# GpSimd adds the squares of four norms, and behind three norms TensorE takes two units together, chunk by chunk

## What is computed

```python
def rms_norm(x, g):
    xf = x.astype(jnp.float32)
    y = xf * lax.rsqrt(jnp.mean(xf * xf, axis=-1, keepdims=True) + EPS)
    return (y * g.astype(jnp.float32)).astype(x.dtype)

def modulate(x, g, shift, scale):
    return rms_norm(x, g) * (1 + scale) + shift
```

## Time and profile before

| What | Value |
|---|---|
| Runs | 2468.7 us median of 3 (2468.6 to 2469.37) |
| The profiled execution's own time | 2463.28 us |
| Its span, first to last instruction | 2461.5 us |
| Mean granted TensorE clock | 0.919 |
| TensorE busy with products | 2011.6 us (82%), 16358 instructions |
| VectorE, ScalarE, GpSimd busy | 909.3, 659.1 and 58.4 us |
| Products of line 524 (sums of squares), all norms | 88 instructions |

### The profile page before, as it was taken

One profiled execution on the slowest core, in us unless ns is written; L12 is line 12 of the kernel. 1 busy time (PEld: TensorE's weight loads), 2 busy tenths in 40 slices (PEclk: granted clock), 3 DMA queues, 4 the chain that ended last, 5 costly groups with the idle time before them and its releaser, 6 DMA issues.

```text
span 2461.5 us, 37332 instructions
## 1 busy us (share of the span) xinstructions
PE 2011.6 (82%) x16358; PEld 1478.3 (60%) x16358; DVE 909.3 (37%) x1620; ACT 659.1 (27%) x1143; POOL 58.4 (2%) x83
## 2 busy tenths in 40 slices
PE   6998898999998998999999997766656666666665
PEld 3896555888776885899898454443333333333332
DVE  2345623434523328466475453322211111111112
ACT  4233414323413326454444301111111111111111
POOL 0010100000000001000010000000000000000000
PEclk8998999999999999999999998888888888888888
DMA  8106841222223231343540153999999999999996
GB/s 330 69 35 249 367 172 69 103 103 82 71 92 125 103 117 47 137 174 140 192 174 9 42 221 137 428 426 427 427 427 427 426 427 427 427 428 426 427 428 292
DMA packets 44544, 592.60 MB, mean 241 GB/s; under 512 B 5549, under 2 KB 5737, under 8 KB 8288
## 3 DMA queue, kind: packets, MB, share of 16 engines
q1 hardware_dynamic: 40608, 579.36, 57.5%
q0 software_dynamic: 2992, 8.96, 1.1%
q10 hardware_dynamic: 784, 1.91, 0.2%
HBM read 589.16 MB, written 1.05 MB: 240 GB/s over the span
## 4 chain that ended last, share of the span: by engine, by line
PE 52%; DMA 28%; DVE 6%; ACT 3%; issue 2%; SPq 0%; DVEq 0%; ACTq 0%
DMA s_ring<-in_w_up 12%; PE bank L539 10%; PE bank L541 10%; PE bank L540 10%; DMA s_arena<-in_w_up 8%; PE bank L1152 5%; DMA s_xT<-in_w_up 4%; DMA s_hT<-in_w_up 3%; PE bank L1166 2%; PE bank L593 1%; PE bank L777 1%; PE bank L582 1%; PE bank L1139 1%; DMA s_ring<-in_slabs 1%; PE bank L765 1%
## 5 line engine op out<-in xcount | busy, mean ns | idle before, releaser
L539 PE MATMUL bank<-s_arena_r 128*128 128x256 f32 (+2 forms) x1656 | 549.6, 332 | 39.3 <-DVE s_hT_r L1842 33.5
L1273 ACT ACTIVATE s_arena<-bank 32x256 f32<-32x256 f32 (+7 forms) x439 | 174.0, 409 | 1079.5 <-PE bank L1152 572.1
L541 PE MATMUL bank<-s_arena_r,s_ring_r 128*128 128x512 f32 (+2 forms) x1312 | 443.9, 338 | 0.0
L1152 PE MATMUL bank<-s_ring,s_arena 128*32 128x256 f32 x2048 | 297.6, 507 | 144.4 <-DMA s_xT<-in_w_up 47.4
L540 PE MATMUL bank<-s_hT_r,s_arena_r 128*128 128x512 f32 (+2 forms) x1096 | 369.8, 337 | 0.0
L539 PEld LDWEIGHTS bank<-s_arena_r 128*128 128x128 f32 x1656 | 315.3, 190 | 79.6 <-issue 37.9
L1837 DVE TENSOR_TENSOR s_ring_r<-s_ring,s_arena_r 128x2048 fp32r<-128x2048 f32 (+1 forms) x96 | 232.4, 2425 | 289.6 <-ACT s_arena_r L1273 289.5
L1152 PEld LDWEIGHTS bank<-s_ring,s_arena 128*32 128x32 f32 x2048 | 145.1, 144 | 220.9 <-issue 207.5
L541 PEld LDWEIGHTS bank<-s_arena_r,s_ring_r 128*128 128x128 f32 x1312 | 252.2, 192 | 27.2
L1273 ACT ACTIVATE s_arena_r<-s_ring 128x2048 fp32r<-128x2048 f32 (+1 forms) x96 | 193.2, 2016 | 138.1 <-PE bank L541 137.3
L2420 DVE TENSOR_TENSOR s_arena<-s_arena,bank 64x256 f32<-64x256 f32 x64 | 27.1, 423 | 543.9 <-ACT s_arena L1273 543.9
(11 more groups left out here) (332 smaller groups left out, 2621.9 us busy)
## 6 DMA issues: line engine op xcount, KB each, us to landing
s_ring<-in_slabs SPq DMA_DIRECT2D x72, 2048.0 KB, 8.2
s_ring<-in_w_down SPq DMA_DIRECT2D x32, 2048.0 KB, 28.9
s_ring<-in_w_up SPq DMA_DIRECT2D x32, 2048.0 KB, 32.9
s_ring<-in_w_gate SPq DMA_DIRECT2D x32, 2048.0 KB, 33.4
s_arena<-in_w_gate SPq DMA_DIRECT2D x16, 2048.0 KB, 33.5
s_arena<-in_w_up SPq DMA_DIRECT2D x16, 2048.0 KB, 34.0
s_arena<-in_w_down SPq DMA_DIRECT2D x16, 2048.0 KB, 28.9
s_ring<-in_slabs SPq DMA_DIRECT2D x16, 1408.0 KB, 6.4
```

The costliest lines, as they stand in the source:

```text
L539: mm(out, w_hi_, x_hi_, start=start, stop=False)
L541: return mm(out, w_lo_, x_hi_, start=False, stop=stop)
L1152: last = mm(pb[b][32 * q:32 * q + 32, 0:256], x[:, c, :], w[q // 2][:, c, 256 * (q % 2):256 * (q % 2) + 256], start=c == 0, stop=c == DC - ...
L1273: return act.activation(out, in_, func, **kw)
```

## The change

GpSimd gets `add_squares`: it adds the squares of chunks 0 to 6 in place of the six products, into memory that is free at that time. `residual_norm` then has two products, one of the total and one of chunk 7, both behind the last unit. ScalarE rounds chunk 0 directly behind its modulation and the others as before. `norm_split` interleaves VectorE's factors and splits, two factors ahead, for n2_0 and n2_1. In `ffn` and `in2` TensorE makes the first two units together: three products for each of them whenever a chunk has come.

```diff
+        def sq_sum(name):
+
+            o = AW - W_HALF if name in ("n2_0", "n2_1") else AW - W_OUT - TT
+            return arena[:, o:o + TT]
...
+            def add_squares(name, T):
+
+                q0, _ = norms[name]
+                total = sq_sum(name)[:, 0:T]
+                for c in range(1, DC - 1):
+                    pool.wait_ge(S["sq_ready"], q0 + c + 1)
+                    if c == 1:
+                        pool.tensor_tensor(total, sq[:, q0 % 2, 0:T], sq[:, (q0 + 1) % 2, 0:T], ALU.add).then_inc(S["sq_used"], 2)
+                    else:
+                        pool.wait_ge(S["sq_used"], q0 + c)
+                        pool.tensor_tensor(total, total, sq[:, (q0 + c) % 2, 0:T], ALU.add).then_inc(S["sq_used"], 1)
+            add_squares("n2_0", TT)
+            add_squares("n1_1", TT)
             pool.wait_ge(S["ffn_out_mm"], DC)
             pool.dma_start(meta, d["metaT"].rearrange("(c p) t -> p c t", p=P)).then_inc(S["meta_in"], 16)
...
+            add_squares("n2_1", NT)
+            add_squares("fin", TT)
             pool.wait_ge(S["ffn_out_mm"], 2 * DC)
...
             def residual_norm(name, m, T):
 
-                if m >= 1:
-                    norm_chunk(name, m - 1, DC, 7, T, 1024)
                 if m == DC - 1:
+                    T = TT if name == "fin" else T
+                    pe.wait_ge(S["sq_used"], norms[name][0] + DC - 1)
+                    mm(pb[7][:, 0:T], ON[1024], sq_sum(name)[:, 0:T], start=True, stop=False)
                     norm_chunk(name, m, DC, 7, T, 1024)
...
+                    if i == 0:
+                        for c in range(DC):
+                            pe.wait_ge(S["h_lo"], DC * (2 * l + 1) + c + 1)
+                            for a in range(2):
+                                last = split_mm(pb[a][:, 0:T], w_hi[0][:, c, a, :], wl[:, c, a, :], h_hi[:, c, 0:T], hT_r[:, c, 0:T],
+                                                c == 0, c == DC - 1)
+                                if c == DC - 1:
+                                    last.then_inc(S["ffn_in_mm"], 1)
+                        continue
...
             def in2(slab, units, name, ev, prev, ahead=0):
-                for u in range(units):
+                first = 0
+                if slab == 0:
+                    first = 2
+                    pe.wait_ge(S["w_lo"], W_IN2 + 1)
+                    wh, wl = w_half[0], half(place_r[FIRST["in2"]], 0)
+                    for c in range(DC):
+                        pe.wait_ge(S["h_lo"], 4 * DC + c + 1)
+                        for u in range(2):
+                            last = split_mm(pb[u][:, 0:T2], wh[:, c, 128 * u:128 * u + 128], wl[:, c, 128 * u:128 * u + 128], h2_hi[:, c, :], h2_lo[:, c, :],
+                                            c == 0, c == DC - 1)
+                            if c == DC - 1:
+                                last.then_inc(S[name], 1)
+                for u in range(first, units):
...
                     last.then_inc(S["mod_h"], 1)
-                    if c >= 1:
+                    if c == 0:
+                        h_rounded(2 * l + which, 0, T)
+                    if c >= 2:
                         h_rounded(2 * l + which, c - 1, T)
                 h_rounded(2 * l + which, DC - 1, T)
...
+            def norm_split(name, k, T):
+
+                rsq(name, T)
+
+                def factor(c):
+                    TTn(hT[:, c, 0:T], xT[:, c, 0:T], rstd[:, 0:T], ALU.mult).then_inc(S["mod_xr"], 1)
+                for c in range(2):
+                    factor(c)
+                for c in range(DC):
+                    if c + 2 < DC:
+                        factor(c + 2)
+                    h_rest(k, c, hT[:, c, 0:T], hT_r[:, c, 0:T], h_hi[:, c, 0:T])
+                dve.sem_inc(S["norm_done"], 1)
...
             def ffn(l, T):
-                for c in range(DC):
-                    h_rest(2 * l + 1, c, hT[:, c, 0:T], hT_r[:, c, 0:T], h_hi[:, c, 0:T])
...
-            norm_mod("n2_0", 1, TT)
+            norm_split("n2_0", 1, TT)
...
-            norm_mod("n2_1", 3, NT)
+            norm_split("n2_1", 3, NT)
```

More of the change, by code:

```diff
@@ L551, in ffn @@
                         for c in range(DC):
-                            if i + a == 0:
-                                pe.wait_ge(S["h_lo"], DC * (2 * l + 1) + c + 1)
                             last = split_mm(pb[b][:, 0:T], w_hi[i % 3][:, c, a, :], wl[:, c, a, :], h_hi[:, c, 0:T], hT_r[:, c, 0:T],
@@ L872, in in2 @@
                     for c in range(DC):
-                        if slab + u == 0:
-                            pe.wait_ge(S["h_lo"], 4 * DC + c + 1)
                         last = split_mm(pb[u % 4][:, 0:T2], wh[:, c, o:o + 128], wl[:, c, o:o + 128], h2_hi[:, c, :], h2_lo[:, c, :],
```

## The result

The changed kernel took **2440.2 us** (median of 4 runs, 2436.5 to 2443.6), the kernel before beside it 2468.8: a ratio of 0.989 with a 95% interval of 0.9878 to 0.9902, 28.6 us less. The forecast was 22.7 us less and 2446.0, and its range, 2443 to 2452, ends 2.8 us above the result. The direction and the mechanism of the change are right; the time is outside.

A forecast was written before the change was run, and what follows sets the result against it. Compute, mainly TensorE, was taken to bound the kernel to about 1540 us, then the expert-weight DMA stream. 18.1 + 3.4 + 1.3 + 0 - 0.1 = 22.7 us saved took 2468.7 to 2446.0; range 2443 to 2452.

The forecast's parts named there:

- The norm products: Four norms' sums of squares: six of eight TensorE products removed in each, all on the path, 18.1 us saved.
- The adds cost nothing: GpSimd's adds of squares in four norms: finished before TensorE's last unit ends, so their price is 0.
- The port rule: VectorE and GpSimd share ports by an exclusive lock; adds could lengthen FFN-output weight splits, 2456.9 us, chance 0.02.
- The pair in the first FFN: First FFN's start: TensorE starts 2.5 us sooner and makes two units together, gain 3.4 us, at most 4.2.
- The second FFN: Second FFN's start, half the columns: gain from the earlier start alone, 1.3 us, ends 0.5 and 2.5.
- Second block's input: Pair of first units there: any saving ends in TensorE's 2.52 us wait for VectorE's second half slab, so 0.
- The expert stream: Expert weights from 1538 us: keeps its 902 us at 426 GB/s and starts sooner; not following fully had chance 0.04.
- Runs of this kernel lie within 0.8 us of each other: Whole kernel: assumed run spread, with 0.2% (5 us) about what a measurement can tell from no change.
- the 5.4 us between median and profiled run: Whole kernel: the median's excess over the profiled run, taken as no part of the change.
- Its unknowns: Likeliest case, 2446.0: pairs between 1 and 5.6 us instead of 4.7, stream 2 us either way, giving 2443 to 2450.
- Theory E: Set for the follow-up runs: the change's fixed part is 23 us; the rest is where TensorE's clock falls between runs.
- The rounding of chunk 0: Modulated norms: ScalarE waits once for its own result, costing 0.1 us at n1_1 and 0 at n1_0.

The follow-up runs named there:

- experiment 6: Changed kernel with the FFNs' first two units one after the other again, split order and earlier rounding kept: 2447.7 us, ratio 0.9927.
- experiment 7: Changed kernel with VectorE's eight factors ahead of the first split again, pair and earlier rounding kept: 2446.8 us, ratio 0.9919.
- experiment 3: Changed kernel with only the pair in the second block's input undone: 2439.8 us, ratio 0.9892.
- all fills: Changed kernel plus unread TensorE products in idle time behind the four norms and around the router, run twice: 2433.8 and 2433.9 us.
- second repeat: Changed kernel run a third time, no edit, on the chip of that call: 2440.8 us, ratio 0.9911.
- experiment 9: Kernel before run again without an edit, for a second trace: 2465.3 us, ratio 0.9998.
- experiment 1: Changed kernel with only GpSimd's adds kept; pair operands, split order and rounding as before the change: 2445.6 us, ratio 0.9919.
- experiment 4: Changed kernel run again without an edit, the first repeat: 2443.4 us, ratio 0.991.
- experiment 2: Changed kernel with the adds undone, a norm product per chunk again; pairs, interleaved factors and earlier rounding kept: 2459.0 us, ratio 0.9972.
- experiment 5: Changed kernel plus unread TensorE products (5, 8, 3 and 5) in idle time behind the four norms only: 2441.1 us, ratio 0.9898.
- experiment 11: Kernel before with all fills, the same unread products at the same places: 2461.8 us, ratio 0.9975.

## Why the prediction was right and wrong

**The norm products: right.** 18.1 us forecast, 18.45 in the first trace, 18.4 in the adds alone and in every repeat. The distance between starts of neighbours gave each price; the largest differences are the GLA layer's piece, 5.32 for 5.16, and neighbourhood attention's, 2.85 for 2.58.

**The adds cost nothing: right.** They take 1.27 to 1.30 us with 512 columns and 0.72 with 256, for the 1.4 I took and the 0 to 1.4 that I left open. In the GLA projection the last is over 5.6 us ahead of chunk 7's product. The port rule that the prediction weighed (the Trainium skill, SBUF — State Buffer, "Who interferes with whom") isn't put to the test by these adds: none runs beside an operation of VectorE with two inputs in SBUF, as the rows' spacing had it. The splits stay at 3.09 us.

**The pair in the first FFN: right, and for the reason given.** 3.41 and 16.8 us behind the factor for 3.4 and 17; 3.48 us for 3.4, 2.8 in the repeat. Experiments 6 and 7 show that the early start alone brings nothing and the pair alone 1.45. The bound of 4.2 that I set from the chunks' pace is nearly met when the clock is kept: 4.0. The traces also show where the clock counts. With the old order the second pair begins 20.25 to 20.27 us behind the factor in four traces with 0 to 5.1 us at half clock in between, so the chunks hide it; with pair and order it begins 16.2 us behind without half clock and 17.5 with 6.2 us of it.

**The second FFN: the direction right, the match partly luck.** 1.36 for 1.3, 1.2 to 1.4 in the repeats, all against the first trace of before. In that trace the second pair begins 10.8 us behind the factor. In the second trace it begins 12.0 behind it, with fills 11.4, and in the adds alone 11.3 (with only 3.4 us at half clock in the one with fills, so the clock isn't all of it). Against those the changed kernel's 9.4 to 9.6 is 1.7 to 2.6 us. The forecast rests on a clock that is back after 3.34 us; the second trace of before has 6.2 us at half clock there.

**Second block's input: right.** 0, by experiment 3 and by the piece of 0.00.

**The expert stream: right in the value, wrong as an unknown.** I gave it 2 us either way, and it moved by 0.26. In no trace did the piece behind the first expert's copy move by more than 1 us.

**What failed is the step behind the range.** "Runs of this kernel lie within 0.8 us of each other" rested on three runs. Seventy-one runs of the kernel before lie between 2462.7 and 2474.6, with a median of 2466.1 and a standard deviation of 2.9; fourteen of the changed one lie between 2436.5 and 2453.4, with 2442.2 and 5.4. Two of my steps went down with it. I took the 5.4 us between median and profiled run as fixed; with the changed kernel it was 3.7. And I took the pieces without a change for equal in two traces, where each has steps of up to 3.4 us from one execution of the same kernel to the next. "Its unknowns: pairs between 1 and 5.6 us instead of 4.7, the stream 2 us either way" has no term for that. The term came out at 3.5 us in the first trace. Of these 1.33 and 1.73 are two stretches of half clock that the first trace of before has and that of after has not (below). The miss of 5.8 us is 0.6 of better pieces, these 3.5 and 1.8 of medians. Pooled, the change is worth 2466.1 - 2442.2 = 23.9 us, 1.2 from the forecast; but the pooled 2442.2 too lies 0.8 outside the range, for the absolute time started from 2468.7. (Within the prediction the unknowns don't add up to its 2450 either: 3.7 us less from the pairs and 2 from the stream make 2451.7. It changes nothing, as the range went to 2452 and was missed at the other end.)

**What the pieces without a change are: the clock, as far as shown.** In short stretches between 340 and 1540 us, together 65 to 85 us of a trace without fills behind the norms, TensorE's granted clock is half. Which stretches they are differs between executions: 1499 to 1502 and 1509 to 1526 in the first trace of before, 1496 to 1527 in the second, where the piece up to the first expert's copy is 3.37 us slower. With all fills 26 to 27 us are left, and the changed kernel's spread falls from 17 to 4 us. At the router the same 32 products take 3.76 and 7.07 us.

The two large steps of the first table have the same cause. For the GLA layer's +1.33, the same 128 products in the scan, before and after:

```profile
310.36 5.37 PE L593 MATMUL bank<-s_ring,s_arena 128*32 128x128 f32 x128
...
310.70 3.70 PE L621 MATMUL bank<-s_ring,s_arena 128*32 128x128 f32 x128
```

The first trace of before is at half clock from 310.8 to 314.2, and its 128 products take 1.67 us longer. The four traces without half clock there (after, its second repeat, experiments 6 and 9) reach the first residual at 360.4 to 360.8, the other ten at 361.3 to 363.5. For the +1.73 ahead of the first scan, the second block's input behind its third unit, before and after:

```profile
1236.00:1240.00 4.00, 4.00 (x22) 4.00 (x21) 3.93 (x6) 0.00 (x0) 4.00 (x9) 0.60 0.97 325
...
1211.00:1215.00 4.00, 4.00 (x34) 4.00 (x33) 3.93 (x6) 0.87 (x2) 4.00 (x9) 1.00 0.95 329
```

From the last norm's copy to the first scan the four traces with no half clock there take 88.9 to 89.1 us (after, its second repeat, experiments 3 and 9), the eight with 3.4 us of it 90.2 to 90.6, and the two with 6.8 us (experiments 1 and 4) 91.5 and 91.7. Half clock just behind the norm costs nothing in this sum, since TensorE then waits for the third unit's weights. Why the clock falls in one place in one execution and in another place in the next is open.

**Theory E in the end.** It holds for the kernels without fills (pieces of 23.3 in the first trace, pooled difference 23.9), with the reservation that only the norm pieces are fixed: the FFN pieces move with the clock too. It doesn't say all: with fills the difference is 27.9, the fills bring the changed kernel 8.4 us and the kernel before 3.4 to 4.3. So about 4 us of what a steady clock gives can be had only with the change in place, 0.9 of it in the two FFN starts (4.05 and 1.7 for 3.48 and 1.36), 1.5 in the second FFN's output, where the late stretch of half clock is missing. The rest isn't placed. The rounding of chunk 0 was not tried by itself; its forecast price of 0.1 us is below what these pieces can show.

## What to carry to other kernels

A product in a back-to-back stretch costs the distance that it puts between its neighbours, and work of that kind can go to an idle engine for nothing as long as its last piece is over before the stretch ends. Taking two units together behind a norm pays in full only if the producer also hands over the first chunk early; the early start alone brought nothing and the pair alone less than half. Before a range is set on a few microseconds, look at several executions of the kernel before: three close runs say nothing of where the clock falls. Before a difference between two traces is put down to an edit, compare the granted clock at the same instructions. A few products into an unused bank in TensorE's pauses are worth trying by themselves.

## What the hardware showed beyond that

The granted clock at the same instructions differs between executions of one kernel: the router's 32 products took 3.76 us in the first trace of the changed kernel, 3.76 in that of before, and 7.07 or 7.08 in experiments 2, 5, 6, 7 and 9, where nothing near them was edited. The Trainium skill, TensorE: Matmul & The Clock Gate, Part 1, has half rate as the default state, which activity lifts; the fills agree, as 15 products in the router's pauses kept the clock at 1.00 from 1490 to 1520 us (experiment 11). It also says that the monitor behind this runs free of the kernel, which would let executions differ by how the program lies against it. No run here shows that.

GpSimd's add of 128x512 in float32 with two inputs took 1.27 to 1.30 us and of 128x256 0.72, steadier than its multiplies of 128x512 beside VectorE's work in the GLA scan, 1264 to 1863 ns.
